# A transformer layer on one core: logits of a later row moved behind the values, in TensorE's order

## The reference, cut to what matters

```python
proj = rms_norm(x, mix_norm_g) @ w_in            # u_a, v_a, q, k, v
y_a = spatial_gating(u_a, v_a, ...)              # 512 features
# y_b: 8 heads of 64, 2 key/value heads, chunks of 64 frames; a chunk sees itself and the one before
logits = einsum(q, k_band) * 64 ** -0.5 + bias   # bias by offset; missing keys are -1e30
m = maximum(max(logits), sink)
p = exp(logits - m)
y_b = (p / (sum(p) + exp(sink - m))) @ v_band
y = concat(rms_norm(y_a, g), rms_norm(y_b, g))
x = x + y @ w_out
h = rms_norm(x, ffn_norm_g)
x = x + (silu(h @ w_gate) * (h @ w_up)) @ w_down
out = rms_norm(x, final_norm_g)
```

## Time and profile before

| | |
|---|---|
| median of 3 runs | 931.95 us (931.64 to 932.1) |
| profiled execution | span 930.2 us from first to last instruction; its own time is not listed apart from the span |
| mean granted TensorE clock | 0.998 of full speed |
| TensorE busy | 921.3 us, 99% |
| VectorE, ScalarE, GpSimd busy | 551.3, 403.6, 329.1 us |

### The profile page before, as it was taken

One profiled execution on the slowest core, in us unless ns is written; L12 is line 12 of the kernel. 1 busy time (PEld: TensorE's weight loads), 2 busy tenths in 40 slices (PEclk: granted clock), 3 DMA queues, 4 the chain that ended last, 5 costly groups with the idle time before them and its releaser, 6 DMA issues.

```text
span 930.2 us, 11930 instructions
## 1 busy us (share of the span) xinstructions
PE 921.3 (99%) x4277; PEld 757.5 (81%) x4277; DVE 551.3 (59%) x812; ACT 403.6 (43%) x833; POOL 329.1 (35%) x344
## 2 busy tenths in 40 slices
PE   9999999999999999999999999999999999999997
PEld 7888888878778878888888888888888888888885
DVE  5655773576677966564553645537446676544753
ACT  6743541465655733333333323333335355434451
POOL 1410000022125288575674765755753100000022
PEclk9999999999999999999999999999999999999999
DMA  9621312312224334726437365273557897656643
GB/s 337 229 79 57 89 41 88 88 46 87 73 98 130 102 114 158 226 77 218 153 108 227 99 195 179 90 241 90 182 179 259 317 394 230 188 198 194 191 138 133
DMA packets 132000, 147.02 MB, mean 158 GB/s; under 512 B 16281, under 2 KB 92645, under 8 KB 131941
## 3 DMA queue, kind: packets, MB, share of 16 engines
q1 hardware_dynamic: 131268, 145.86, 48.3%
q10 hardware_dynamic: 672, 0.40, 0.1%
HBM read 105.73 MB, written 40.50 MB: 157 GB/s over the span
## 4 chain that ended last, share of the span: by engine, by line
PE 94%; issue 2%; DVE 2%; DMA 1%; ACT 0%; POOL 0%; DVEq 0%; POOLq 0%; ACTq 0%
PE ps L703 30%; PE ps L705 29%; PE ps L704 29%; PE ps L830 1%; PE ps L849 1%; PE ps L907 1%; PE ps L840 1%; PE ps L779 1%; DMA A22s<-in_w_gate 1%; DVE P_lo L1703 0%; DMA small<-in_mix_gT 0%; DVE T_lo L1690 0%; PE ps L733 0%; PE ps L736 0%; PE ps L739 0%
## 5 line engine op out<-in xcount | busy, mean ns | idle before, releaser
L1703 DVE TENSOR_TENSOR P_lo<-P_raw,P_hi 128x512 fp32r<-128x512 f32 x132 | 118.1, 910 | 82.5 <-ACT P_hi L1227 75.2
L703 PE MATMUL ps<-T_hi,P_hi 128*128 128x512 f32 x352 | 137.1, 389 | 0.0
L705 PE MATMUL ps<-T_hi,P_lo 128*128 128x512 f32 x352 | 136.9, 389 | 0.0
L704 PE MATMUL ps<-T_lo,P_hi 128*128 128x512 f32 x352 | 136.9, 389 | 0.0
L703 PE MATMUL ps<-rb_hi,ra_hi 128*128 128x512 f32 x308 | 119.8, 389 | 0.0
L704 PE MATMUL ps<-rb_lo,ra_hi 128*128 128x512 f32 x308 | 119.8, 389 | 0.0
L705 PE MATMUL ps<-rb_hi,ra_lo 128*128 128x512 f32 x308 | 119.8, 389 | 0.0
L647 POOL TENSOR_TENSOR wd<-wd 128x256 f32<-128x256 f32 x88 | 82.9, 942 | 95.0 <-DMA wd<-in_w_down 89.9
L1328 ACT ACTIVATE ra_hi<-ra 128x512 fp32r<-128x512 f32 x77 | 48.6, 632 | 98.3 <-DMA rb<-w_down_T 58.1
L1783 DVE TENSOR_TENSOR ra_lo<-ra,ra_hi 128x512 fp32r<-128x512 f32 x77 | 56.2, 730 | 37.6 <-ACT ra_hi L1328 37.3
L1227 ACT ACTIVATE P_hi<-P_raw 128x512 fp32r<-128x512 f32 x132 | 76.6, 620 | 3.5 <-POOL P_raw L607 3.5
(11 more groups left out here) (208 smaller groups left out, 1911.4 us busy)
## 6 DMA issues: line engine op xcount, KB each, us to landing
wd<-in_w_down SPq DMA_DIRECT2D x44, 256.0 KB, 3.3
w_down_T<-wd SPq DMA_DIRECT2D x22, 512.0 KB, 5.0
ra<-act_S SPq DMA_DIRECT2D x44, 256.0 KB, 2.7
rb<-w_down_T SPq DMA_DIRECT2D x44, 256.0 KB, 3.0
act_S<-Q SPq DMA_DIRECT2D x33, 256.0 KB, 3.7
ra<-act_A SPq DMA_DIRECT2D x33, 256.0 KB, 5.0
rb<-in_w_down SPq DMA_DIRECT2D x33, 256.0 KB, 5.9
P_raw<-in_w_gate SPq DMA_DIRECT2D x22, 256.0 KB, 3.7
```

The costliest lines, as they stand in the source:

```text
L703: mm(dst, lhs[0], rhs[0], start=start, stop=False, skip_group_check=onto)
L704: mm(dst, lhs[0], rhs[1], start=False, stop=False, skip_group_check=onto)
L705: return mm(dst, lhs[1], rhs[0], start=False, stop=stop, skip_group_check=onto)
L1703: tt(w_l[p, m][:], src[:], w_h[p, m][:].bitcast(F32), ALU.subtract).then_inc(w_split, 1)
```

## The change

On TensorE alone, L(r+3) now stands directly behind V(r+1) in passes r = 0 to 4, and no longer between Y(r) and H(r-1,0). To begin with this, L(1) stands behind P(0,0), V(0) behind O(0,0) with L(2) behind it, and pass 0 runs O(1,1) between P(1,0) and P(1,1), and O(0,2) ahead of V(1). The queues of all other engines stay as they are.

```diff
             probs_T(0, 0)
+            logits(1)
             unit(NQ1 + 3)
             probs_T(0, 1)
-            logits(1)
-            values(0)
...
             out_unit(0, 0)
+            values(0)
+            logits(2)
             out_unit(0, 1)
             out_unit(1, 0)
             probs_T(1, 0)
-            logits(2)
+            out_unit(1, 1)
             probs_T(1, 1)
             yb_rows(0)
             for r in range(T):
...
                     probs_T(r + 1, 1)
                     yb_rows(r)
-                if 0 < r < T - 2:
-                    logits(r + 2)
                 if r + 1 < T:
                     if 0 < r < T - 2:
                         h2_transposed(r - 1, 0)
-                    out_unit(r + 1, 1)
+                    if r:
+                        out_unit(r + 1, 1)
+                    else:
+                        out_unit(0, 2)
                     if r == T - 2:
                         h2_transposed(r - 1, 0)
                     values(r + 1)
+                    if r + 3 < T:
+                        logits(r + 3)
                     if 0 < r < T - 2:
                         h2_transposed(r - 1, 1)
-                out_unit(r, 2)
+                if r:
+                    out_unit(r, 2)
```

## The result

The changed kernel takes 944.91 us (median of 4 runs, 944.11 to 945.46) against 931.98 us (median of 4) for the kernel before on the same chips: a ratio of 1.0139, 95% interval 1.0124 to 1.0153, or 12.9 us slower. I had said 940.6, in a range of 938.0 to 943.2. The direction and both mechanisms were there; the loss is half as large again as I made it.

The account below looks back on a forecast made before the run. TensorE, busy 99% of 930.2 us, was taken as the bound. Delays of 6.24 us up to P(2,0), 0.51 in pass 1 and 2.10 in later passes made 8.85, taken as 8.7: 940.6 us, range 938.0 to 943.2.

Parts of the forecast that it names:

- both mechanisms: Moved work no longer covers other chains: x2n 0.83 us late for H, w_out's pieces 3.15 us late for O(0,2).
- The wait of O(0,2) for woB_split: In pass 0, TensorE idles 3.15 us before the third k-piece and 0.5 before the fourth; 3.8 us lost.
- The wait of H for x2n: Passes 1 to 5: TensorE idles 0.60 us once and 0.89 us four times, 4.2 us in all.
- the likeliest case: Whole kernel: the forecast of 940.6 us with its own bounds, 939.3 to 942.3 us.
- a rival: TensorE's clock falls in the idle time at O(0,2); half rate loses 1.6 or 3.2 us, 942.2 to 943.8; chance 0.09.
- parts 1 and 2: Loop: logits leave their place before H and follow V; a pass with both edits is 0.80 us longer.
- Part 1: Loop: without the logits before H, H waits 0.89 us for x2n; everything behind comes 0.30 us earlier.
- part 5: P(2,0) and pass 1: P(2,0) comes 6.24 us later, pass 1 is 0.51 us longer.
- only part 4: Only O(0,2)'s wait counts, x2n coming early enough: 4.5 us slower, 936.5 us; chance 0.04.
- only parts 1, 2, 3 and 5: All but O(0,2)'s wait counts, its pieces being ready before Y(0): 4.9 us slower, 936.9 us; chance 0.03.
- not slower: Whole kernel: earlier logits save 5 shape changes and waits at P(2,0) and P(7,0), 930.6 us; chance 0.03.
- The changes of shape: TensorE's switches between tile shapes: 31 before, 26 after, about 0.16 us each, 0.8 us saved.

Follow-up runs that it names:

- Experiment 3: Changed kernel with 26 and 4 unused transposes of the identity ahead of the third and fourth k-pieces of O(0,2), waits kept: 943.46 us, ratio 1.0124.
- experiment 5: The kernel of experiment 1 with GpSimd's first sum of y_b's squares also waiting for VectorE's reciprocal of the same pass: 936.24 us, ratio 1.0041.
- experiment 1: Kernel before with only the loop's logits moved behind the values, old order ahead of the loop and of pass 0: 938.37 us, ratio 1.0069.
- experiments 5 and 8: The second of the two: changed kernel with the same added GpSimd wait for VectorE's reciprocal as in experiment 5: 943.20 us, ratio 1.0114.
- experiment 6: The kernel of experiment 1 with H(r-1,0) moved behind O(r+1,1) in passes 1 to 5: 932.24 us, ratio 1.0000.
- experiment 2: Kernel before with only the changed order up to O(0,2), without L(3), and the old order from pass 1 on: 940.18 us, ratio 1.0085.
- experiment 4: Changed kernel with woB_piece(2) and (3) ahead of yb_totals(0), add_bias(2) and maxima(2) on VectorE: 941.51 us, ratio 1.0101.

## Why the prediction was wrong

**Held.** The wait of O(0,2) for woB_split: 3.03 and 0.23 us of idle array in the trace, 4.71 us between Y(0) and the third piece. The wait of H for x2n, five times, 5.4 us by the weight loads and 4.2 us of idle array, the sum that I had; but it agrees by luck, as the five are 0.72, 1.13, 0.77, 0.79 and 0.77 us, where I had 0.60 and four times 0.89. P(1,0) at 185.40, 2.19 us later than in the earlier trace rows (0.65 of which is this execution's late start), where I had 1.69; it waits for normal_probs(1), as said. Pass 5 shorter, by 0.4 us, for which I had 0.3. The rest of the kernel hands the delay on: P(7,0) comes 13.5 us later (285.09 for 271.57), and the span is 13.5 us longer.

**Failed, first: the likeliest case kept the full clock.** P(2,0) was put at +6.24 us and came at 203.14 - 194.90 - 0.65 = +7.6. The difference is the half rate behind the 3.03 us of idle time, which I had as a rival, priced at 1.6 us with a chance of 0.09. Experiment 3 measures 1.5. The argument against it, that no row of before shows a fall, was empty: there was no such pause between two matmuls to show one. And the end of the same trace does show a fall. The last matmul ends at 923.23 + 0.39 = 923.62, the clock is at 1.00 until 926 and at 0.50 from there on:

```profile
926.00:927.00 1.00, 0.00 (x0) 0.00 (x0) 0.66 (x1) 0.00 (x0) 0.30 (x1) 0.50 0.62 254
```

The half rate that the rival took from the earlier trace rows rests on the pace of the transposes alone; the granted clock of 1.51 to 4.75 reads 1.00 there. The Trainium skill (TensorE: Matmul & The Clock Gate, Why this matters for your kernels) warns of idle gaps between bursts of matmuls, as they bring the half rate back, and the trace now agrees, with 0.53 in one window.

**Failed, second and larger: "parts 1 and 2 together +-0.1 a pass", in Part 1's words on what stands ahead of add_out(r,3) on VectorE: "They hang on add_out(r,2) and so on PE, and move with it."** They move in relation to GpSimd too, which stays where it was. From one P(r+1,0) to the next, passes 1 to 4 took 15.32, 15.32, 15.26 and 15.27 us before and 1.26, 1.67, 1.38 and 1.36 us more after, where the sum had 0.51 and 0.80 three times: 2.8 us too little. Of these the collision is 2.3 us: without it, in experiment 5, the four passes take 16.06, 16.41, 16.06 and 16.06 us, where experiment 1 has 16.58, 16.99, 16.64 and 16.64. In the rows it is 0.50 us in the small addition and 0.10 in the multiplication behind it, and the medians of experiments 5 and 8 give 1.7 to 2.5 for the whole. Where nothing collides, passes 3 and 4 are 0.80 us longer than before, the forecast to the digit. The margin could be read before: VectorE's addition at 238.95 and GpSimd's sum at 239.65 leave 0.70 us, and my own sum moved the one by 0.80 us.

**Failed, third and small: the chain of x2n in passes 1 and 2.** The slack ahead of H was 0.36 us in pass 3, but in pass 2 of the same trace x2n ended at 213.86 + 1.28 = 215.14 and H started at 215.20:

```profile
212.85 0.55 POOL L561 TENSOR_TENSOR late<-late,small 128x1 f32<-128x1 f32 x1
...
213.86 1.28 DVE L1653 SCALAR_TENSOR_TENSOR x2n<-xr,late,ffn_gB 128x1024 f32<-128x1024 f32 x1 [2.58 <-POOL late L561]
...
215.20 0.65 PE L907 MATMUL ps<-ident,x2n 128*128 128x128 f32 x4
```

VectorE starts there 0.46 us behind the root and not 0.10, in both kernels. That is the 0.3 us by which pass 2 exceeds passes 3 and 4. Why it starts late stays open. In pass 1, part 5 counted x2n's chain from add_out(0,3), but ScalarE's copy of P(2,0)'s transposes stands ahead of the squares in its queue: the squares start at 204.33, 1.19 us behind P(2,0), and H(0,0) at 207.82, 4.68 us behind it where I had 4.39.

The terms: 8.7 as forecast, 1.4 for the clock, 2.8 for the passes (2.3 the collision, 0.5 the third point), makes 12.9, which is what was measured. **Of the rivals**, "only part 4" falls by experiment 1 (the loop alone costs 6.3), "only parts 1, 2, 3 and 5" by the 3.03 us of idle time, "not slower" by all of these. The changes of shape are real in the starts (0.20 for 0.11 us in the earlier trace rows), but their worth was only argued: experiment 6, with fewer of them, comes out at 1.0000. Its passes 1 to 5, by the windows:

```profile
195.88:271.62 75.74, 74.68 (x431) 59.96 (x431) 51.71 (x85) 45.77 (x140) 16.09 (x29) 1.00 0.22 77
```

TensorE is busy for 74.68 us there; with 1.10 us for the L that isn't among them that is 0.8 us less than the 76.59 us of before, or 0.14 us for each of the six changes of shape that these passes have fewer, near the 0.16 that I had. But it is also idle for 1.06 us, 0.91 of it in pass 5 in front of a second H that has no L as cover, and this takes the gain back. Busy times are modelled, so this is a reading and not a measurement.

No variant beats the kernel before. What its order may give away in changes of shape it has back as cover: L between Y and H covered x2n's chain, O(1,1) and V(1) between Y(0) and O(0,2) covered w_out's last pieces.

## What to carry to other kernels

Where one engine is busy throughout, each group of instructions in its queue is also a cover: before moving one, list the chains that end behind it, with their slack in every pass and not in one. A shift between engines that share something reorders them even where no semaphore ties them, so compare the shift with the margin between their starts; a short instruction that comes second pays for the long one. And an idle time of TensorE like this one of 3.03 us is to be priced with the half rate behind it, or filled; the end of a trace, where TensorE has nothing left to do, can show whether the clock falls at all.

## What the runs showed of the hardware that was not expected

- An 8-element addition on VectorE took 0.66 us instead of 0.16 when GpSimd's 128x256 sum had started 0.09 us before it. Starting GpSimd behind it, by an added wait, took 2.1 us off the kernel.
- The granted clock fell to the 1.2 GHz level for 3.4 us behind an idle time of 3.03 us, not in it but 0.9 us after TensorE had started again (0.7 us in experiment 2, behind 3.04 us). Pauses of 0.7 to 1.1 us in the passes and one of 2.21 us in experiment 4 left it at 1.00. With 30 transposes of the identity in the pauses, it stayed at 1.00.
- TensorE's shapes: V(1) of 8 matmuls took 1.73 us in the slow stretch and 1.01 us outside, while the L behind it ran at full rate again (1.10 us).
